# Second layer's gate modulation moved between the layers, second weight tile loaded last, low-weight parts between the row tiles

## The chip, the cores and the metric

One Trainium2 chip, one core of it. The kernel is one launch that computes the whole step. The metric is the device time of the launch in microseconds, lower is better.

## The reference

Two layers of a decoder trunk, over one prompt of 512 rows and eight decode rows (520 rows together), model width 1024. Cut to what matters:

```
for l in range(2):
    mod = silu(c) @ ada_w[l] + ada_b[l]            # (9, 3072): 1 prompt + 8 decode vectors
    shift, scale, gate = split(mod, 3)             # 1024 each
    h = rms_norm(x, norm_g[l]) * (1 + scale) + shift
    proj = h @ w_in[l]                             # 1024 x 7944
    oA, oB, oC, oD = four mixer branches of proj's first columns   # each 256 wide
    up = stack([oA, oB, oC, oD]) @ w_up[l]         # four products to width 1024
    merged = sum_n(sigmoid(proj gate columns n) * up_n)
    x = x + gate * (merged @ w_out[l])
y = rms_norm(x, final_g)
```

`shift` and `scale` of a layer are needed before its first product; `gate` is needed only where the layer's output is added to x.

## The kernel before, in words

All activations lie transposed: 128 of the 1024 (or 256) channels on the partitions, the 520 rows along the free axis. A "row tile" below is one of the KT = 8 groups of 128 channels of h. Each product of w_in and w_out is done in parts for precision: a weight tile (128 output columns, 1024 deep, 512 KB) is loaded into a ring of three places (`ring`, filled by SP), ScalarE copies it to a rounded high part (`w_hi`, `split`, `first_split`), GpSimd computes the low part (`w_lo`). h has a high part (`h_hi`, ScalarE) and a low part (`h_lo`, VectorE). `product` then has 12 parts (PARTS) for one weight tile: parts 0 to 7 take row tile p with the high weights against h_hi and h_lo (four matmuls), parts 8 to 11 take the low weights of two row tiles against h_hi (four matmuls). After the last part ScalarE evacuates the bank (`evac`) and splits the tile two places further on.

Order on every engine is written out by hand: each engine has one instruction stream, and named semaphore tracks (`STEPS`, at the end of the file) count its steps. All transfers of a layer go through SP's one queue, in the order of the list `L.tiles`. A layer does the projections, the four branches (their small products are mixed with the remaining projection and gate tiles), then a tail: `up` 18 to 31, and eight output tiles `out` 0 to 7. The tanh of each gate tile is written out to memory and brought back (`scr_tanh`) for its `up`; the weights of an up (`upw`, 128 KB) are in a ring of three, reloaded when an up is done (`load_up`).

The modulation: silu(c) is in `c32`. A piece of `ada_w` is 256 rows by 512 columns (512 KB, in the ring); `ada_products` multiplies it with c32 (four fp32 matmuls), four pieces make one set of 512 columns, ScalarE copies the sums out (`modrow`) and `mod_columns` turns them into columns of the modulation. Layer 0's shift and scale are computed at the start (`ada0`, `mod0`, blocks 0 to 3 of 2 MB each in places of their own, in the order 0, 2, 1, 3, the first two giving the first half of the channels). Layer 0's tail holds 24 pieces: eight for its own gate, one after each of up 20, 22, 24, 26, 28, 29, 30 and 31, and sixteen for layer 1's shift and scale, two or three after each of the output tiles 0 to 5. Layer 1's tail holds eight, for its own gate, after the same ups.

At the start of layer 0, SP issues blocks 0 and 2, weight tile 0, block 1, weight tile 1, block 3, weight tile 2 and then x's save and the constants. TensorE takes block 0 and 2, their columns, block 1, and then goes through row tiles 0 to 3 for weight tiles 0 and 1 side by side, block 3, the columns, the first two low parts of both weight tiles, row tiles 4 to 7, and the rest of the low parts. ScalarE splits weight tiles 0 and 1 before it computes the first h_hi. In layer 1 the eight row tiles are followed by all low parts.

Between the layers: after output tile 7 come the sum of squares (`square_sums`, in two parts), its logarithm and exponential on ScalarE, and the first row tile on VectorE and ScalarE.

Of the kernel before, what the change touches and what calls it, by code (L numbers as in the profile page):

```python
# [18 lines left out]
P = 128  # L19
# [58 lines left out]
def build_program(nc, a, o, order):  # L78
# [8 lines left out]
    with ctx:  # L87
# [112 lines left out]
        s_ada0 = [sem(f"ada_in{c}") for c in range(8)]  # L200
        pe0, act0, dve0 = (track(n) for n in ("pe0", "act0", "dve0"))
# [19 lines left out]
        class Layer:  # L221

            def __init__(self, n):
# [15 lines left out]
                self.n_ada = 24 if n == 0 else 8  # L239
                self.up_piece = {k: m for m, k in enumerate((20, 22, 24, 26, 28, 29, 30, 31))}  # L240
# [37 lines left out]
        LAND = [RA[:, 2], RA[:, 3], ws[:, 16], ws[:, 17]]  # L278

# [107 lines left out]
        def _(sp):  # L387
# [23 lines left out]
            ada_loads(1)  # L411
            first_load(sp, 1, LAYERS[0], 0)
            ada_loads(3)
# [13 lines left out]
        def _(act):  # L427
# [15 lines left out]
            first_split(act, 1, LAYERS[0])  # L443
# [28 lines left out]
        def _(pe):  # L472
# [35 lines left out]
            ada0(pe, 2)  # L508


        for layer, L in enumerate(LAYERS):
# [53 lines left out]
            def _(sp):  # L565
# [63 lines left out]

                def load_up(n):  # L630
# [23 lines left out]
                def before(kind, n):  # L654
# [47 lines left out]
                    elif (kind, n) == ("ada", 2):  # L702
# [7 lines left out]
                    elif (kind, n) == ("ada", 5):  # L710
# [4 lines left out]
                if layer == 0:  # L715
                    sp.wait_ge(s_zero, 2)
                    sp.wait_ge(*pe0.at("mod", 3))
                sp.dma_start(srow[:, :], a["state_rows"][layer]).then_inc(s_st, 16)
# [10 lines left out]
                for x in L.tiles:  # L729
# [192 lines left out]
            def _(pe):  # L922
# [100 lines left out]
                pe.wait_ge(*ap.at("proj", 9))  # L1023
                crow_rows([RA[:, j] for j in range(7)], 0, 0, pa.step("crow"))
# [495 lines left out]

                def turn(d):

                    pe.wait_ge(*dve_f.at("xg", d))
# [42 lines left out]
                for e in range(KT):  # L1566
# [7 lines left out]
                    if layer and e == 0:  # L1574
                        mods(1)
# [6 lines left out]
                if layer == 0:  # L1582
# [1181 lines left out]
```

## Time and profile before

| what | value |
|---|---|
| three runs | 1366.55, 1369.79, 1371.92 us; median 1369.79 |
| the profiled execution | 1368.49 us, span 1366.6 us |
| mean granted TensorE clock | 0.987 |
| TensorE busy | 1318.0 us, 96% of the span |
| VectorE busy | 623.3 us, 46% |
| ScalarE busy | 450.7 us, 33% |
| GpSimd busy | 375.0 us, 27% |
| DMA queue of SP | 159.00 MB, 42.6% of 16 engines |

The span is the time from the first to the last instruction of the profiled execution; its own time is that with what lies around it. Shares of busy time are averages over stages that differ. Names of engines in the rows: PE is TensorE (PEld its weight loads), DVE VectorE, ACT ScalarE, POOL GpSimd, SPq the queue of the engine that issues transfers. A row's bracket gives the idle time of the engine before the instruction and what ended it.

### The profile page before, as it was taken

The page shows a single profiled execution, that of the slowest core. Times are in us where ns is not written, and L with a number is a line of the kernel's source. Part 1 is how long each engine was busy: PE and PEld are TensorE (multiplying, and loading weights), DVE is VectorE, ACT ScalarE, POOL GpSimd, SP SyncE. Part 2 cuts the span into 40 slices and gives each one's busy share as a digit, 9 for nine tenths or more (in the row PEclk, how much of TensorE's full clock was granted, in tenths as well). Part 3 has the DMA queues.
Part 4 walks back from the last instruction along what each step waited for, and adds up shares of the span by engine and source line. Part 5 has one row for each costly group of instructions (what it writes and reads, how often), then busy time and mean ns, then how long its engine had stood idle before and what let it go on. Part 6 is the DMA issues. An engine that isn't in the chain of part 4 may idle for free.

```text
span 1366.6 us, 39992 instructions
## 1 busy us (share of the span) xinstructions
PE 1318.0 (96%) x18150; PEld 1190.6 (87%) x18150; DVE 623.3 (46%) x1166; ACT 450.7 (33%) x742; POOL 375.0 (27%) x286
## 2 busy tenths in 40 slices
PE   5899999999999999999989999999999999999996
PEld 4799999889899999887779999999988899988796
DVE  3557524317234336756252961332643242565643
ACT  3334422234322235231243353222442223532223
POOL 0244422223222232220333452212331222322121
PEclk9899999999999999999999999999999999999998
DMA  9833231216331272578853433212373224545932
GB/s 309 265 89 93 68 93 49 65 49 138 106 86 49 65 141 78 159 195 260 286 170 79 106 78 82 62 35 70 76 165 96 52 57 92 126 133 134 290 120 94
DMA packets 275932, 162.59 MB, mean 119 GB/s; under 512 B 86102, under 2 KB 244922, under 8 KB 275252
## 3 DMA queue, kind: packets, MB, share of 16 engines
q1 hardware_dynamic: 275220, 159.00, 42.6%
q8 instruction: 143, 2.34, 0.7%
q10 hardware_dynamic: 544, 1.05, 0.2%
q14 instruction: 25, 0.20, 0.0%
HBM read 135.25 MB, written 24.89 MB: 117 GB/s over the span
## 4 chain that ended last, share of the span: by engine, by line
PE 90%; DMA 3%; DVE 2%; ACT 2%; SPq 2%; issue 1%; ACTq 0%; DVEq 0%
PE psA L942 40%; PE psA L950 20%; PE psA L992 8%; PE psB L884 2%; PE psB L868 2%; DMA ring<-in_ada_w 2%; PE psB L888 1%; PE psB L1073 1%; PE psB L315 1%; PE psB L1083 1%; DMA ring<-in_w_in 1%; SPq L400 1%; PE psB L852 1%; PE psB L1311 1%; PE psB L800 1%
## 5 line engine op out<-in xcount | busy, mean ns | idle before, releaser
L778 POOL TENSOR_TENSOR w_lo<-ring,w_hi 128x512 fp32r<-128x512 f32 x248 | 331.1, 1356 | 823.6 <-ACT w_hi L1607 779.1
L942 PE MATMUL psA<-h_hi,w_hi 128*128 128x260 f32 x1984 | 426.8, 297 | 10.4 <-DVE h_lo L2034 9.4
L942 PE MATMUL psA<-h_lo,w_hi 128*128 128x260 f32 x1984 | 401.9, 284 | 0.8 <-issue 0.8
L942 PEld LDWEIGHTS psA<-h_hi,w_hi 128*128 128x128 f32 x1984 | 307.4, 190 | 30.4 <-issue 19.1
L942 PEld LDWEIGHTS psA<-h_lo,w_hi 128*128 128x128 f32 x1984 | 308.7, 190 | 1.4 <-issue 1.1
L950 PE MATMUL psA<-h_hi,w_lo 128*128 128x260 f32 x1984 | 273.6, 286 | 0.0
L950 PEld LDWEIGHTS psA<-h_hi,w_lo 128*128 128x128 f32 x1984 | 249.0, 187 | 6.8 <-issue 3.0
L1607 ACT CAST w_hi<-ring 128x1024 fp32r<-128x1024 f32 x120 | 123.9, 1032 | 10.0 <-DMA ring<-in_w_in 9.9
L893 ACT COPY ws<-psB 128x128 f32<-128x128 f32 x80 | 21.4, 268 | 190.0 <-PE psB L868 162.6
L1637 ACT ACTIVATE tg<-psA 128x520 f32<-128x520 f32 x48 | 28.9, 602 | 119.5 <-PE psA L950 119.3
L901 DVE COPY_PREDICATED tg<-tmask,psB 128x128 f32<-128x128 uint8 x40 | 14.2, 355 | 102.6 <-PE psB L888 58.9
L901 DVE COPY_PREDICATED ws<-tmask,psB 128x128 f32<-128x128 uint8 x40 | 14.2, 356 | 79.2 <-PE psB L888 42.6
L778 POOL TENSOR_TENSOR rb_lo<-RB,w_hi 128x512 fp32r<-128x512 f32 x16 | 21.7, 1380 | 98.4 <-ACT w_hi L1607 98.4
L778 POOL TENSOR_TENSOR rb_lo<-RB,ra_lo 128x512 fp32r<-128x512 f32 x16 | 21.0, 1338 | 49.1 <-ACT ra_lo L1607 49.1
L992 PE MATMUL psA<-RB,upw 128*128 128x260 f32 x128 | 31.8, 393 | 1.7 <-DVE psA L2100 0.9
L1622 ACT COPY RA<-psA 128x520 f32<-128x520 f32 x18 | 10.7, 593 | 64.0 <-PE psA L950 64.0
L992 PEld LDWEIGHTS psA<-RB,upw 128*128 128x128 f32 x128 | 23.2, 190 | 9.5 <-issue 4.9
L2300 DVE SCALAR_TENSOR_TENSOR ws<-RD,parT,ws 128x511 f32<-128x511 f32 (+2 forms) x36 | 30.9, 924 | 0.7 <-ACT ws L1810 0.6
L992 PE MATMUL psA<-RA,upw 128*128 128x260 f32 x128 | 30.7, 385 | 0.0
L992 PE MATMUL psA<-RD,upw 128*128 128x260 f32 x128 | 29.9, 384 | 0.8 <-DVE RA L2101 0.8
L992 PE MATMUL psA<-RC,upw 128*128 128x260 f32 x128 | 30.0, 387 | 0.3 <-DVE psA L2100 0.3
L950 PE MATMUL psA<-merged_hi,rb_lo 128*128 128x260 f32 x224 | 29.1, 282 | 0.0
(504 smaller groups left out, 1973.3 us busy)
## 6 DMA issues: line engine op xcount, KB each, us to landing
ring<-in_w_in SPq DMA_DIRECT2D x122, 512.0 KB, 4.3
ring<-in_ada_w SPq DMA_DIRECT2D x32, 512.0 KB, 5.9
scr_tanh<-tg SPq DMA_DIRECT2D x48, 260.0 KB, 4.6
upw<-in_w_up SPq DMA_DIRECT2D x64, 128.0 KB, 3.5
RB<-in_w_out SPq DMA_DIRECT2D x16, 512.0 KB, 3.8
RA<-scr_tanh SPq DMA_DIRECT2D x30, 260.0 KB, 3.8
ws<-scr_tanh SPq DMA_DIRECT2D x24, 260.0 KB, 4.2
xT<-scr_x SPq DMA_DIRECT2D x8, 520.0 KB, 4.7
```

The lines of the kernel that those rows point to most:

```text
L315: last = nc.tensor.matmul(out[g:g + 32, 0:256], c32[:, k0 + k, :], piece[:, k, 256 * f:256 * f + 256], start=start, stop=stop)
L778: nc.gpsimd.tensor_tensor(tile_part(RL[s][:, k], (kind, n)), tile_part(RS[s][:, k], (kind, n)), tile_part(HS[L.hslot[q]][:, k], (kind, n)) ...
L868: last = nc.tensor.matmul(meet(z0[pr, cols], lv, 0), At[pr, q, cols], meet(T4[pr, q, cols], lv, 0), start=True, stop=True)
L884: nc.tensor.matmul(meet(z0[pr, cols], lv, 0), V4[pr, q, cols], meet(Y4[pr, q, cols], lv, 0), start=True, stop=True)
L893: nc.scalar.copy(meet(q64(Y), lv, 0), meet(q64(psB[:, 2, 0:256]), lv, 0)).then_inc(*ta.step("y"))
L901: nc.vector.copy_predicated(meet(q64(T), lv, 0), bc(meet(tmask[:, lv, :], lv, 0), 1, 4), meet(q64(psB[:, 2, 0:256]), lv, 0))
L942: nc.tensor.matmul(out(h), HS[L.hslot[q]][:, p, 0:m], cols(part(p), h), start=(p == 0 and part is hi), stop=False)
L950: last = nc.tensor.matmul(out(h), RL[s][:, k, 0:m], cols(hi(k), h), start=False, stop=(k == KT - 1))
L992: last = nc.tensor.matmul(out(hf), upw[:, idx % UP_RING, i, :], outs[MERGE[idx][0]][:, i, hf * HALF:(hf + 1) * HALF], start=(i == 0), stop ...
L1607: nc.scalar.copy(tile_part(HS[L.hslot[q]], SPLIT[q]), tile_part(RS[s], SPLIT[q])).then_inc(*aw.step("hi"))
L1637: A(half(th_tile(idx)), psA[:, b:b + 2, 0:HALF], ACT.Tanh, scale=0.5).then_inc(*am.step("th"))
L2300: last = STT(out[:, t, sh:SEQ], raw[:, t, 0:SEQ - sh], par(wname, tap * n + t), out[:, t, sh:SEQ], mult, add)
```

## The change

Five edits, in one.

1. Start of layer 0: SP issues the fourth modulation block (block 3) ahead of weight tile 1. ScalarE splits tile 1 only after it has copied out the last two blocks' sums, so after the first half's h_hi. TensorE takes row tiles 0 to 3 for weight tile 0 alone, then blocks 1 and 3 and the columns, then two low parts of tile 0, row tiles 0 to 3 of tile 1 and its two low parts.
2. In both layers the low parts of the first two weight tiles come between the row tiles: after every second row tile, the part that needs the two.
3. Layer 1's tail has no pieces of `ada_w` any more. SP loads them in layer 0's tail, into places of their own (`LATE`, eight places of 1024 columns): two after up 15, two after up 20, one after up 25, three after output tile 0, as soon as that place is free.
4. TensorE multiplies them at layer 0's end: two before the sum of squares, six behind it. ScalarE copies the sums in layer 1 after h_hi, TensorE forms the columns after the first two weight tiles, VectorE adds the bias and halves them before the projections' shift.
5. Small stores that stood with pieces 2 and 5 in layer 1 go to output tiles 2 and 3; SP's first loads of layer 1 wait for the last late piece.

```diff
+        LATE = [two(t, at) for t, at in ((ws, 10), (RC, 2), (RB, 6), (ws, 0), (RC, 0), (RB, 4), (RA, 2), (ws, 16))]
+        late_bank = lambda b: psB[:, 1 - b, 0:256]
+        late_mods = psB[:, 0, 256:512]
-                self.n_ada = 24 if n == 0 else 8
+                self.n_ada = 24 if n == 0 else 0
...
             ada_loads(1)
+            ada_loads(3)
             first_load(sp, 1, LAYERS[0], 0)
-            ada_loads(3)
             first_load(sp, 2, LAYERS[0], 0)
...
             first_split(act, 0, LAYERS[0])
-            first_split(act, 1, LAYERS[0])
...
             mod0(pe, 1)
-            ada0(pe, 2)
...
+                def load_late(*ms):
+                    for m in ms:
+                        sp.dma_start(wide(LATE[m]), a["ada_w"][1, 256 * (m % 4):256 * (m % 4) + 256, 2048 + 512 * (m // 4):2560 + 512 * (m // 4)]
+                                     .rearrange("(k p) c -> p k c", p=P)).then_inc(s_late[m], 16)
...
-                    elif (kind, n) == ("ada", 2):
+                    elif (kind, n) == (("ada", 2) if layer == 0 else ("out", 2)):
...
-                    elif (kind, n) == ("ada", 5):
+                    elif (kind, n) == (("ada", 5) if layer == 0 else ("out", 3)):
...
+                else:
+                    sp.wait_ge(*LAYERS[0].TR["pe_f"].at("ada", 31))
                 sp.dma_start(srow[:, :], a["state_rows"][layer]).then_inc(s_st, 16)
...
+                    if layer == 0 and x == ("up", 15):
+                        sp.wait_ge(*dn.at("gated", 2))
+                        load_late(0, 1)
+                    if layer == 0 and x == ("up", 20):
+                        sp.wait_ge(*dn.at("gated", 3))
+                        load_late(2, 3)
+                    if layer == 0 and x == ("up", 25):
+                        sp.wait_ge(*pm.at("gate", 23))
+                        load_late(4)
+                    if layer == 0 and x == ("out", 0):
+                        sp.wait_ge(*merged_at(31))
+                        load_late(5, 6, 7)
...
-                for p in range(KT):
-                    if layer == 0 and p == KT // 2:
-                        ada0(pe, 3)
-                        mod0(pe, 2)
-                        mod0(pe, 3)
+                if layer == 0:
+                    proj(0, range(KT // 2))
+                    ada0(pe, 2)
+                    ada0(pe, 3)
+                    mod0(pe, 2)
+                    mod0(pe, 3)
+                    proj(0, (KT, KT + 1))
+                    proj(1, range(KT // 2))
+                    proj(1, (KT, KT + 1))
+                for p in range(KT // 2 if layer == 0 else 0, KT):
+                    for idx in range(2):
+                        proj(idx, [p])
+                    if p % 2:
                         for idx in range(2):
-                            proj(idx, (KT, KT + 1))
-                    proj(0, [p])
-                    proj(1, [p])
-                for idx in range(2):
-                    proj(idx, range(KT + 2 if layer == 0 else KT, PARTS))
+                            proj(idx, [KT + p // 2])
+                if layer:
+                    for b in range(2):
+                        pe.wait_ge(*LAYERS[0].TR["act_f"].at("modrow", 6 + b))
+                    for b in range(2):
+                        mod_columns(late_mods, b, modrow[:, b, :]).then_inc(*LAYERS[0].TR["pe_f"].step("mod"))
...
+                def late(m):
+                    pe.wait_ge(s_late[m], 16)
+                    if m == 4:
+                        pe.wait_ge(*dve_f.at("mod2"))
+                        pe.wait_ge(*dve_f.at("parT"))
+                    ada_products(late_bank(m // 4), wide(LATE[m]), 2 * (m % 4), m % 4 == 0, m % 4 == 3).then_inc(*pe_f.step("ada"))
...
-                    if layer and e == 0:
-                        mods(1)
...
                 if layer == 0:
+                    late(0)
+                    late(1)
                     square_sums().then_inc(*pe_f.step("ss"))
+                    for m in range(2, 8):
+                        late(m)
...
                         mod_rows0(act, 3)
+                        first_split(act, 1, LAYERS[0])
...
+                if layer:
+                    for b in range(2):
+                        act.wait_ge(*LAYERS[0].TR["pe_f"].at("mod", 4 + b))
+                        act.wait_ge(*LAYERS[0].TR["pe_f"].at("ada", 27 + 4 * b))
+                        nc.scalar.copy(modrow[:, b, :], late_bank(b)).then_inc(*LAYERS[0].TR["act_f"].step("modrow"))
                 evac(0, 1)
...
+                if layer:
+                    f0 = LAYERS[0].TR
+                    dve.wait_ge(*f0["pe_f"].at("mod", 7))
+                    did(f0["dve_f"], "modT", T_(modT[:, 16:24, :], late_mods[:, 0:72].rearrange("p (r s) -> p r s", r=8), bc(par("ada_b", 16, 8), 2, 9), add), 1)
+                    did(f0["dve_f"], "gate", S_(modT[:, 16:24, :], modT[:, 16:24, :], 0.5, None, mult), 1)
                 dve.wait_ge(*ap.at("proj", 9))
```

## Rows read from the trace of the kernel before

**Rows 1.** The page's part 4: share of the chain by line.
```profile
PE psA L942 40%; PE psA L950 20%; PE psA L992 8%; PE psB L884 2%; PE psB L868 2%; DMA ring<-in_ada_w 2%; PE psB L888 1%; PE psB L1073 1%; PE psB L315 1%; PE psB L1083 1%; DMA ring<-in_w_in 1%; SPq L400 1%; PE psB L852 1%; PE psB L1311 1%; PE psB L800 1%
```

**Rows 2.** Busy time by stretch: length, PE, PEld, DVE, ACT, POOL, clock, DMA share, GB/s.
```profile
606.50:646.80 40.30, 39.27 (x250) 28.60 (x249) 24.51 (x36) 9.89 (x15) 4.97 (x4) 1.00 0.82 259
646.80:700.30 53.50, 51.38 (x468) 45.16 (x468) 16.51 (x39) 12.60 (x18) 20.12 (x14) 1.00 0.84 280
1269.40:1308.00 38.60, 37.61 (x234) 28.27 (x232) 24.41 (x36) 9.89 (x15) 4.96 (x4) 1.00 0.72 233
```

**Rows 3.** Chain of waits, 20 to 60 us: start, length, what.
```profile
21.97 12.39 DMA ring<-in_w_in
...
35.33 0.72 ACT h_hi L1683
...
37.19 5.92 PE psA L942 x32
...
44.98 1.13 PE psB L322 x8
...
50.34 0.67 DVE h_lo L2034
...
58.41 1.68 PE psA L942 x12
```

**Rows 4.** Timeline of layer 0's start: start, length, engine, line, operation.
```profile
29.20 0.75 DVE L2044 SCALAR_TENSOR_TENSOR hT<-RC,G,tg 128x512 f32<-128x512 f32 x1
...
32.64 1.93 PE L315 MATMUL psB<-RB,cond_padded 128*32 128x256 f32 x16 [1.71 <-DMA RB<-in_ada_w]
...
49.73 0.51 PE L942 MATMUL psA<-h_hi,w_hi 128*128 128x260 f32 x2 [1.63 <-DVE h_lo L2034]
```

**Rows 5.** Busy time by stretch, as rows 2, where the clock is down.
```profile
32.00:36.00 4.00, 1.93 (x16) 0.59 (x16) 0.00 (x0) 1.62 (x3) 0.00 (x0) 0.50 1.06 377
...
52.00:56.00 4.00, 4.00 (x24) 4.00 (x24) 1.86 (x6) 0.42 (x1) 0.00 (x0) 0.63 1.07 205
...
705.00:710.00 5.00, 1.27 (x6) 1.30 (x7) 4.64 (x9) 2.30 (x4) 0.85 (x1) 0.69 0.39 103
```

**Rows 6.** Timeline between the layers, TensorE.
```profile
702.40 1.14 PE L1538 MATMUL psB<-ws,cst 128*128 128x260 f32 x4 [1.10 <-ACT ws L1986]
...
708.73 0.77 PE L942 MATMUL psA<-h_hi,w_hi 128*128 128x260 f32 x2 [5.18 <-DVE h_lo L2034]
...
718.75 3.99 PE L950 MATMUL psA<-h_hi,w_lo 128*128 128x260 f32 x32
...
722.58 0.45 PE L942 MATMUL psA<-h_hi,w_hi 128*128 128x260 f32 x2
```

**Rows 7.** Timeline of layer 1's tail.
```profile
1289.56 3.77 PE L992 MATMUL psA<-RB,upw 128*128 128x260 f32 x16
...
1293.58 0.70 DVE L2100 SCALAR_TENSOR_TENSOR psA<-RA,psA 128x520 f32<-128x520 f32 x1
...
1301.84 1.94 PE L1550 MATMUL psA<-merged_hi,ra_lo 128*128 128x260 f32 x14
```

**Rows 8.** Layer 0's tail: stretches; the transfer issued at 614.60; timeline, chain; waits.
```profile
585.00:587.50 2.50, 2.50 (x24) 2.30 (x22) 1.14 (x3) 0.00 (x0) 0.00 (x0) 1.00 0.04 3
650.00:652.50 2.50, 2.50 (x23) 2.50 (x22) 0.00 (x0) 0.77 (x2) 2.19 (x2) 1.00 0.99 369
...
upw<-in_w_up SPq DMA_DIRECT2D x1, 128.0 KB, 4.1
...
618.88 1.99 PE L992 MATMUL psA<-RB,upw 128*128 128x260 f32 x8
...
646.95 6.94 DMA ring<-in_ada_w
...
654.50 0.51 PE L942 MATMUL psA<-merged_hi,w_hi 128*128 128x260 f32 x2
...
PE psB L315 <- DMA ring<-in_ada_w: 1.9, 4, 0.7
```

More of the change, by code:

```diff
@@ L200, in build_program @@
         s_ada0 = [sem(f"ada_in{c}") for c in range(8)]
+        s_late = [sem(f"late_ada_in{m}") for m in range(8)]
         pe0, act0, dve0 = (track(n) for n in ("pe0", "act0", "dve0"))
@@ L238, in __init__ @@
                     "pe_n", "act_n", "dve_n", "pe_m", "act_m", "dve_m")}
-                self.n_ada = 24 if n == 0 else 8
-                self.up_piece = {k: m for m, k in enumerate((20, 22, 24, 26, 28, 29, 30, 31))}
+                self.n_ada = 24 if n == 0 else 0
+                self.up_piece = {k: m for m, k in enumerate((20, 22, 24, 26, 28, 29, 30, 31)) if m < self.n_ada}
                 self.out_pieces = [[m for m in pieces if m < self.n_ada] for pieces in
@@ L1023, in _ @@
                 pe.wait_ge(*ap.at("proj", 9))
+                if layer:
+                    pe.wait_ge(*LAYERS[0].TR["dve_f"].at("gate", 1))
                 crow_rows([RA[:, j] for j in range(7)], 0, 0, pa.step("crow"))
@@ L1519, in _ @@
                         ada(L.up_piece[idx])
+                def late(m):
[4 more added lines that the diff above has]
+                    ada_products(late_bank(m // 4), wide(LATE[m]), 2 * (m % 4), m % 4 == 0, m % 4 == 3).then_inc(*pe_f.step("ada"))
                 def turn(d):
+                    if d == 0:
+                        pe.wait_ge(*TR["act_c"].at("hrow"))
                     pe.wait_ge(*dve_f.at("xg", d))
@@ L2130, in _ @@
                 did(dd, "gc", v.tensor_tensor_scan(bg[32:36, :], cc("reset", 32, 36), g1, 0.0, mult, add))
+                if layer:
+                    f0 = LAYERS[0].TR
+                    dve.wait_ge(*f0["pe_f"].at("mod", 7))
+                    did(f0["dve_f"], "modT", T_(modT[:, 16:24, :], late_mods[:, 0:72].rearrange("p (r s) -> p r s", r=8), bc(par("ada_b", 16, 8), 2, 9), add), 1)
+                    did(f0["dve_f"], "gate", S_(modT[:, 16:24, :], modT[:, 16:24, :], 0.5, None, mult), 1)
                 dve.wait_ge(*ap.at("proj", 9))
@@ L2530, in _ @@
                 mods = lambda lo, n: psB[:, 0, 9 * lo:9 * (lo + n)].rearrange("p (r s) -> p r s", r=n)
-                dve.wait_ge(*pe_f.at("mod", 1))
-                did(dve_f, "modT", T_(modT[:, 16:24, :], mods(0, 8), bc(par("ada_b", 16, 8), 2, 9), add))
-                did(dve_f, "gate", S_(modT[:, 16:24, :], modT[:, 16:24, :], 0.5, None, mult))
+                if layer == 0:
+                    dve.wait_ge(*pe_f.at("mod", 1))
+                    did(dve_f, "modT", T_(modT[:, 16:24, :], mods(0, 8), bc(par("ada_b", 16, 8), 2, 9), add))
+                    did(dve_f, "gate", S_(modT[:, 16:24, :], modT[:, 16:24, :], 0.5, None, mult))
                 def sum_squares(k):
@@ L2603 @@
     'dve0': 'c_zero silu_c xs c parT selh hrows spread x x x x x x x x ssp modT G modT G sel tmask'.split(),
-    'pe_f0': 'st ada ada ada ada ada ada mod ada ada ada ada mod ada ada ada ada mod ada ada ada ada mod ada ada ada ada mod ada ada mod par ss'.split(),
-    'act_f0': 'hh hhd hh hh hh hh hhd hh hh hh lam_abs lam_z expA modrow modrow sq modrow sq modrow sq sq modrow sq modrow sq sq sq lnx rs'.split(),
-    'dve_f0': 'hg hr hs hd hs hld hl hs hl hs hl hl hg hr hs hd hs hld hl hs hl hs hl hl zero der lam1 lam2 lam3 lam4 lam5 lamm13 lama13 lamm11 lama11 lamm9 lama9 lamm7 lama7 lamm5 lama5 lamm3 lama3 lamm1 lama1 lam6 lam_y lam_sp stT modT gate acc acc acc acc acc acc parT mod2 G'.split(),
+    'pe_f0': 'st ada ada ada ada ada ada mod ada ada ada ada mod ada ada ada ada mod ada ada ada ada mod ada ada ada ada mod ada ada mod par ada ada ss ada ada ada ada ada ada mod mod'.split(),
+    'act_f0': 'hh hhd hh hh hh hh hhd hh hh hh lam_abs lam_z expA modrow modrow sq modrow sq modrow sq sq modrow sq modrow sq sq sq lnx rs modrow modrow'.split(),
+    'dve_f0': 'hg hr hs hd hs hld hl hs hl hs hl hl hg hr hs hd hs hld hl hs hl hs hl hl zero der lam1 lam2 lam3 lam4 lam5 lamm13 lama13 lamm11 lama11 lamm9 lama9 lamm7 lama7 lamm5 lama5 lamm3 lama3 lamm1 lama1 lam6 lam_y lam_sp stT modT gate acc acc acc acc acc acc parT mod2 G modT gate'.split(),
     'pe_a0': 'crow lora lora kks kkb bsum gram gram tr tr z gram y z y z gram y z y z tr y tr z z gram y x1 z u y o z gram y x1 z u y o z tr y tr z z gram y x1 z u y o z gram y x1 z u y o z tr y tr z z y x1 z u y o z y x1 z u y o z y z x1 u o x1 u o mt'.split(),
```

6 lines of the change are left out of this document (3 added, 3 removed).

## Prediction

> **What bounds the kernel now.** I read the chain of waits first: it runs through TensorE almost all the way, most of it the projection's products of line 942 and their low-weight parts of line 950 [rows 1]. So a change counts only by what it adds to or takes from TensorE's queue, and by the waits in that queue. Then I read the busy time by stage. In layer 0's tail TensorE is busy 39.3 of 40.3 us and 51.4 of 53.5 us, with the DMA engines at 0.82 and 0.84; in layer 1's tail 37.6 of 38.6 us, DMA 0.72 [rows 2]. TensorE's queue is therefore full, but layer 0's tail has little DMA to spare. Last I read three places where it does stand still: the start, the step between the layers, and single waits for transfers in the tails.
>
> **Start of layer 0.** The chain goes through the landing of the second weight tile at 34.36 (issued 21.97, 12.39 us); ScalarE then splits it, and only at 35.33 starts the first h_hi, though VectorE had written that row tile at 29.95 [rows 3, 4]. The change takes this split out of the way: h_hi starts at about 30.1, 5.3 us earlier, and the first product at 31.9 instead of 37.19. VectorE paces the row tiles at 1.33 us (two operations of 0.67 [rows 3]), so tile 0's first four parts are through at 36.3. Only then does TensorE take the third block of the modulation. Half a block takes 1.93 us at the low clock (0.50 from 32 to 36 [rows 5], x16 in 1.93 [rows 4]), so 0.97 at the high one. With the clock back soon after 38, the third block ends near 39.2 and the fourth near 41.2; its data land some 1.7 us earlier, being now ahead of a 512 KB tile. ScalarE's copy and the last columns take 1.1 us (44.98 + 1.13 = 46.1 before [rows 3]), so they end at 42.3, 3.8 us earlier. VectorE and ScalarE then need 3.6 us until the second half's first row tile (46.1 to 49.73 [rows 3, 4]), to 45.9. TensorE fills this: low parts of tile 0 (8 matmuls of 0.12 [rows 6], 0.96), four parts of tile 1 (1.93), its low parts (0.96), to 46.2. Four row tiles for two weight tiles (3.9) and two pairs of low parts (1.9) end at 52.0. Both tiles now end together, so evacuation and split of the third tile (1.9 us after the first tile's end, measured between the layers: 718.75 + 2.0 to 722.58 [rows 6]) lie open for 1.3 us: the third tile starts at 53.3 against 58.41 [rows 3], 5.1 us earlier. If the clock stays low until 41.3, as it did, it is 3.7. I take 4.8; ends 3.0 and 5.5. The tile "ba" is then asked for behind the masks and state rows that are still landing; it is wanted at 59.1, which I cost at nothing, 1 us if that cover fails.
>
> **Layer 1's tail.** Out go eight pieces of the gate modulation among the last ups, two sets of columns, and two small VectorE operations before the first output tile (beside the products, nothing). Pitch of two ups without a piece: 3.77 us from 1289.56 with the tail of the last matmul in it [rows 7], so 1.83 to 1.85 each. Fourteen ups by 1.83 are 25.6; out_first from 1301.84 to its end at about 1307.7 is 5.85. Together 31.5 of the 38.6 us of this stretch [rows 2], a gain of 7.1. VectorE is late next: in the last ups it has three operations of 0.7 per up [rows 7], some 2.0 us with their overlap against 1.83, about 0.3 us in all that shows. An up's weights must now land within 3.6 us of their issue; without the pieces nothing queues ahead of them. I take 6.8, ends 5.5 and 7.3. Four small stores that SP issued beside pieces 2 and 5 move ahead of the third and fourth output tiles, issued before their wait ends: nothing.
>
> **Between the layers.** Eight pieces at 0.48 (half of a half block's 0.97) are added. Two go before the square sums into TensorE's wait of 1.10 us for the last square, six into the wait of 5.18 us for h_lo [rows 6]; both hide them. SP's state loads wait for the last piece, 4 us; what follows on SP is next wanted at about 720, so nothing. Then the low parts come between the row tiles: the stretch of 64 high and 32 low matmuls is 11.5 us at the high clock from 708.73, 720.2, plus the open 1.4 of evacuation and split (the columns, 0.8, lie in it): the third tile at 722.0 against 722.58, a gain of 0.6. But the work is now bound by TensorE's clock instead of by VectorE. The clock was down here (0.69 [rows 5]), and it was down from 52 to 56 (0.63 [rows 5]) after an idle of only 1.63 us before 49.73 [rows 4]; 2.2 us of idle remain now. Some 3 us at the low clock, as there, cost 1.5. I take a loss of 0.8, ends a gain of 0.7 and a loss of 2.
>
> **Layer 0's tail pays.** The 4 MB that layer 1's tail no longer loads are loaded here: eight loads of 512 KB. At 369 GB/s [rows 8] one takes 1.4 us of all DMA engines.
> - Pieces 0 and 1, near 581, go into an almost idle DMA (0.04 [rows 8]): nothing.
> - Pieces 2 and 3, after up 20 (612.5), stand ahead of the weights of up 24. These were issued at 614.60, took 4.1 us to 618.7, and up 24 began at 618.88 [rows 8]: no slack. 2.8 us less a little idle: 2.6.
> - Piece 4, after up 25: slack of 1 us and more in the ups behind: 0.3.
> - Pieces 5 to 7, after output tile 0, go ahead of the ring's pieces 11 and 12. The latter landed at 646.95 + 6.94 = 653.89 and the next tile's products began at 654.50 [rows 8]: no slack, 4.2 us. In exchange later waits shrink: there are 1.9 us of them for pieces [rows 8], of which 1.1 come back: 3.1.
> - Both standstills are longer than the 1.63 us after which the clock fell [rows 4], so I add 1.5 for matmuls at half rate; ends 0 and 3.
> Sum 7.5, ends 3 and 10.
>
> What row and rule say on the queue: the latencies in this tail grow with what was issued just before (4.1 us for 128 KB, 6.94 for 512 KB behind three others [rows 8]). The Trainium skill, page "DMA: Bandwidth & Descriptors", section "Two DMAs through the same engine are not ordered", has descriptors within one queue of one engine start in order. By that rule no small load passes a late piece, and the stalls stand; if small loads passed, the cost would be near nothing, which is the first rival. This speaks against the change, and the trace agrees.
>
> **Sum.** Against the profiled execution (1368.49, of which 1366.6 span and 1.9 around it): -4.8 - 6.8 + 0.8 + 7.5 = -3.3, 1365.2. The median of the three runs is 1.3 above it; from 1369.79 I forecast 1366.5.
>
> **Rivals.**
> 1. The late loads are hidden: then 3.3 + 7.5 = 10.8 us are gained, 1359.0. For it: DMA is not full (0.82). Against it: the landings that end just before their use.
> 2. The start gives only about 1.5 us: the third and fourth blocks now run after products at the low clock and the clock stays low to the last columns, or "ba" or the masks come late. Gain 3.3 less 3.3: 1369.8. For it: clock 0.50 from 32 to 36 [rows 5]. Against it: TensorE is busier there than before.
> 3. Slower: late loads starve the output tiles. This phase refills three ring places per tile; if the 4.2 us of backlog is never worked off, so that every following group of pieces waits for it again, each of three more groups costs some 3 us, 9 in all with half-rate matmuls: 1366.5 + 9 = 1375.5. It decides once a group's loads are issued less than 7 us before use (6.94 was the landing). Against it: a standing TensorE lets the DMA drain, and no wait for a piece was longer than 0.7 us before [rows 8].
> 4. The tail of layer 0 costs 4 instead of 7.5: no clock loss, and DMA works off a part of each backlog while TensorE is at the matmuls before. 1363.0.
>
> **Chances.** Forecast 0.55, rival 1 0.12, rival 2 0.13, rival 3 0.05, rival 4 0.15. Half a per cent, 6.8 us, is about what a measurement tells from no change here. Faster by more (below 1362.9): rival 1, half of rival 4 and a little of the forecast, 0.24. Slower by more (above 1376.6): part of rival 3, 0.04. Within: 0.72. Range 1360.5 to 1371.0: it leaves out most of rival 1 and rival 3.
>
> **What would show it.** Right: first L942 product near 32; third tile's first product near 53; no L315 in layer 1's tail, which ends its first output tile about 7 us sooner after up 18; TensorE idle near up 24 of layer 0 waiting for upw, and 3 to 4 us after output tile 1 waiting for ada_w, with a lower granted clock behind them. Wrong: no such waits (rival 1), or the columns' end in layer 0 later than 44 (rival 2), or idle of over 2 us in each output group (rival 3).

## The result, and the profile after

Changed kernel: 1373.64 us median of 9 runs (1371.6 to 1377.1); the kernel before beside it 1370.35 (1366.27 to 1372.41, 9 runs). Ratio 1.0038, 95% interval [1.0023, 1.0054]: slower by 5.2 us (3.2 to 7.4, at 1370 us). Forecast were 1366.5, range 1360.5 to 1371.0: outside, and on the other side. The profiled execution took 1372.27 us (span 1370.5) against 1368.49 and 1366.6. Busy times hardly moved (TensorE 1318.5 us against 1318.0), so the question is again one of waits and of the clock.

The chain of waits by engine. In the kernel before TensorE had 90% of it, VectorE 2% and DMA 3%: VectorE's share has grown. The products of lines 942 and 950 in [rows 1] are lines 964 and 972 now:

```profile
PE 88%; DVE 4%; DMA 3%; ACT 2%; SPq 1%; issue 1%; ACTq 0%; DVEq 0%
```

To see where the time went, take the same instruction in both traces and subtract its starts. The same was done for every experiment; the table gives the difference to the profiled execution before, in us (its own time in the first row). "Third tile" is its first product, "up 20, 31" are layer 0's ups, "squares" the first matmul of the square sums, "L1" layer 1's first product, "stT" VectorE's copy of that name in layer 1, "crow" the transposes of crow_rows in layer 1, "lora" the product behind them, "up 17'" and "out 0'" an up and the first output product of layer 1's tail, "end" the last matmul.

```
                       third        up    up                                 up      out
                       tile         20    31  squares  L1    stT  crow  lora  17'     0'    end
before (time)          58.4        610   637   700     709   746   770   782  1254   1302   1357
the change             -0.4       -2.3  -0.1  +5.3    +4.3  +3.7  +6.1  +7.6 +11.2   +4.7   +3.8
e1 gate early          -2.4       -1.8  +0.3  +7.6    +6.5  +7.4  +7.4  +7.4 +10.6   +3.8   +2.9
e2 late loads short    -0.7       -2.3  -3.6  -0.8    -1.9  -0.8  +1.5  +3.0  +7.4   +0.7   -0.3
e3 start undone        -1.5       -4.0  -0.3  +5.9    +4.8  +5.5  +7.9  +9.4  +9.8   +3.0   +2.0
e4 split first         -4.5       -4.0  -0.1  +5.7    +4.7  +5.4  +7.7  +9.2 +12.6   +6.0   +5.0
e5 late loads moved    -2.1       -2.2  -2.2  +2.4    +1.3  +1.9  +4.2  +5.8  +8.6   +1.7   +0.8
e6 e1 + e4 + e5        -4.9       -4.2  -3.6  +3.7    +2.7  +2.1  +2.1  +2.1  +3.8   -3.3   -3.5
e7 start alone         -2.2       -3.9  -4.2  -3.9    -3.9  -3.9  -3.9  -3.9  -4.6   -4.0   -4.0
e8 start alone, split  -4.0       -4.3  -4.6  -5.5    -5.5  -5.6  -5.6  -5.6  -6.2   -6.4   -6.9
e9 e1 + e4, spread     -4.3       -5.9  -6.0  -1.3    -2.3  -1.3  -1.3  -1.3  +0.8   -6.2   -7.1
e10 e9, low parts last -4.6       -0.9  -2.0  +2.9    +1.9  +2.6  +2.6  +2.6  +4.5   -2.5   -3.4
e11 e1 + e4, short     -4.4       -3.6  -4.1  -2.9    -4.0  -4.5  -4.5  -4.5  -3.1  -10.0  -10.6
e12 e9, old start      -0.8        0.0  +0.2  +8.3    +7.2  +6.7  +6.7  +6.7  +8.2   +1.2   +0.3
```

One profiled execution carries much chance, above all by where the clock falls: e9 and e10 run the same instructions up to layer 1 and stand 5.0 us apart at up 20; e3 and e12 have the kernel before's instructions up to up 15, and e3 is 4.0 us early at up 20 where e12 is at 0.0. So single entries are read together with the ratios below, or over several kernels at once.

**Start.** The timeline, as [rows 4]:

```profile
33.15 0.77 PE L964 MATMUL psA<-h_hi,w_hi 128*128 128x260 f32 x2 [3.73 <-DVE h_lo L2085]
43.78 1.31 DVE L385 SCALAR_TENSOR_TENSOR G<-modT,parT 128x36 f32<-128x36 f32 x1
43.76 2.52 POOL L800 TENSOR_TENSOR w_lo<-ring,w_hi 128x512 fp32r<-128x512 f32 x2 [4.65 <-ACT w_hi L307]
45.12 1.20 DVE L2092 TENSOR_TENSOR hT<-mg,G 128x32 f32<-128x32 f32 x1
49.17 0.51 PE L964 MATMUL psA<-h_hi,w_hi 128*128 128x260 f32 x2 [1.84 <-DVE h_lo L2085]
57.99 0.47 PE L964 MATMUL psA<-h_hi,w_hi 128*128 128x260 f32 x2 [1.24 <-ACT w_hi L1652]
```

The first product comes 4.0 us earlier (37.19 in [rows 3]), the third tile 0.4 (58.41 there). In between VectorE's G takes 1.31 us and hT 1.20; the same two took 0.20 and 0.19 before. Over all profiles (the table's first column) the third tile starts at 56.9 to 58.4 with the old start (the kernel before, e3, e12), at 56.0 to 58.0 with the new one (the change, e1, e2, e5, e7) and at 53.5 to 54.4 with the new one and ScalarE's swap of e4 (e4, e6, e8 to e11). By the means the new start is worth 0.8 us there, and 3.7 with the swap.

**Layer 0's tail.** The stretches of [rows 2], then the 4 us behind output tile 1, the waits from 600 to 705 us (total, times, longest), and the products that waited behind output tile 1:

```profile
608.00:648.50 40.50, 37.16 (x247) 27.37 (x247) 24.52 (x40) 6.17 (x11) 4.25 (x4) 1.00 0.88 294
648.50:704.00 55.50, 50.21 (x448) 43.74 (x448) 14.96 (x34) 12.60 (x18) 20.03 (x14) 0.97 0.85 287
...
657.00:661.00 4.00, 3.21 (x20) 2.39 (x19) 0.00 (x0) 1.82 (x3) 0.33 (x1) 0.57 1.09 363
```

```profile
PE psB L319 <- DMA ring<-in_ada_w: 5.3, 4, 3.1
PE psA L1014 <- DMA upw<-in_w_up: 1.8, 2, 1.1
PE psA L1014 <- DVE mg L2152: 1.6, 1, 1.6
```

```profile
656.37 0.64 PE L319 MATMUL psB<-ring,cond_padded 128*32 128x256 f32 x8 [3.13 <-DMA ring<-in_ada_w]
657.80 1.08 PE L319 MATMUL psB<-ring,cond_padded 128*32 128x256 f32 x8 [0.79 <-DMA ring<-in_ada_w]
```

Waits for pieces were 1.9 us in four, at most 0.7 [rows 8]; now 5.3 in four, at most 3.1, and the granted clock was 0.57 over the 4 us behind them: at the lower level of 1.2 GHz for most of the stretch, at 2.4 GHz for the rest.

**Between the layers** (as [rows 6]): the idle of 5.18 us is 2.48 now, and the clock stays high there. The first two late pieces stand ahead of the squares and the other six behind them; the second part of the squares, which waited 1.10 us for ScalarE before [rows 6], starts without a wait:

```profile
705.60 1.14 PE L1578 MATMUL psB<-ws,cst 128*128 128x260 f32 x4
706.65 1.14 PE L1581 MATMUL psB<-ws,cst 128*128 128x260 f32 x4
...
713.00 0.48 PE L964 MATMUL psA<-h_hi,w_hi 128*128 128x260 f32 x2 [2.48 <-DVE h_lo L2085]
...
724.87 0.96 PE L326 MATMUL psB<-sel_halves,ws 128*128 128x18 f32 x8
```

So the squares stand 5.3 us late, and 1.1 us of that is given back at once: their second part, and layer 1's first product, are 4.2 to 4.3 us late. In the table every kernel with late pieces shows this step of 1.1 us between "squares" and "L1", and e7 and e8, without them, do not. What layer 0's tail cost is therefore read at "L1".

**A new wait before crow_rows.** The chain of waits at 770 to 780 us, after (start, length, what):

```profile
773.64 1.24 DVE bg L2181
774.91 0.24 DVE modT L2186
...
775.17 1.11 DVE modT L2187
776.28 0.14 issue
776.42 1.26 PE psB L1021 x7
```

and the same place in the timeline of the kernel before, where TensorE's crow_rows (line 999) did not need VectorE's long chain and ran beside its last operation:

```profile
769.91 1.23 DVE L2130 TENSOR_TENSOR_SCAN bg<-cst,small_rows 4x520 f32<-4x520 f32 x1
...
770.37 0.93 PE L999 MATMUL psB<-cst,RA 128*11 128x128 f32 x7
```

The columns of the late gate modulation (`late_mods`) lie in the PSUM bank that crow_rows writes. So TensorE must wait until VectorE has read them, and VectorE reads them only behind a chain of 26 operations, most on small_rows. TensorE waits 2.2 us, and then the clock is low from 776.9 to 780.3 (0.66 below).

```profile
776.00:781.00 5.00, 4.58 (x26) 4.41 (x27) 4.93 (x6) 0.94 (x2) 1.44 (x2) 0.66 0.22 61
```

**Layer 1's tail** (as [rows 7]): no pieces stand among the ups any more. Up 17 is 11.2 us later than before, and out_first, the first output tile, only 4.7.

```profile
1293.83 12.76 PE L1014 MATMUL psA<-RB,upw 128*128 128x260 f32 x53
1306.53 1.94 PE L1593 MATMUL psA<-merged_hi,ra_lo 128*128 128x260 f32 x14
```

### The profile page after: what moved, and what is told of

The parts are those of the page before. It is cut to its first block, busy times and chain, and to the rows that moved or that the text cites. A ratio compares the mean times of both kernels' runs of the same rounds, so it can differ in the third digit from the quotient of the medians.

```text
span 1370.5 us, 40001 instructions
## 1 busy us (share of the span) xinstructions
PE 1318.5 (96%) x18150; PEld 1192.8 (87%) x18150; DVE 624.1 (46%) x1166; ACT 450.6 (33%) x742; POOL 373.8 (27%) x286
## 4 chain that ended last, share of the span: by engine, by line
PE 88%; DVE 4%; DMA 3%; ACT 2%; SPq 1%; issue 1%; ACTq 0%; DVEq 0%
PE psA L964 38%; PE psA L972 19%; PE psA L1014 7%; PE psB L890 2%; PE psB L906 2%; PE psB L910 1%; DMA ring<-in_ada_w 1%; PE psB L1106 1%; PE psB L319 1%; PE psB L1116 1%; DMA upw<-in_w_up 1%; PE psB L874 1%; PE psB L1344 1%; DMA hT<-in_x_prompt 1%; PE psB L1069 1%
```

## The experiments

Twelve kernels. Ratios are to runs of the kernel before on the same chip, and different groups ran on different chips, so the ratios are compared and not the medians.

| kernel | median us | ratio to before, 95% |
|---|---|---|
| the change | 1373.64 | 1.0038 [1.0023, 1.0054] |
| e1 gate early | 1371.14 | 1.0013 [0.9999, 1.0026] |
| e2 late loads short | 1366.42 | 0.9977 [0.9962, 0.9992] |
| e3 start undone | 1375.23 | 1.0042 [1.0027, 1.0057] |
| e4 split first | 1373.71 | 1.0027 [1.0009, 1.0045] |
| e5 late loads moved | 1369.87 | 1.0013 [0.9996, 1.0030] |
| e6 = e1 + e4 + e5 | 1360.91 | 0.9937 [0.9917, 0.9958] |
| e7 start alone, on before | 1365.79 | 0.9983 [0.9968, 0.9998] |
| e8 start alone, split first | 1366.24 | 0.9977 [0.9964, 0.9990] |
| e9 = e1 + e4, late loads spread | 1361.53 | 0.9945 [0.9928, 0.9962] |
| e10 = e9, layer 1's low parts last | 1362.66 | 0.9952 [0.9929, 0.9975] |
| e11 = e1 + e4, late loads short | 1361.35 | 0.9952 [0.9935, 0.9970] |
| e12 = e9 with the old start | 1366.85 | 0.9969 [0.9953, 0.9985] |

**e1: the new wait.** The two operations ahead of VectorE's long chain:

```diff
+                if layer:
+                    f0 = LAYERS[0].TR
+                    dve.wait_ge(*f0["pe_f"].at("mod", 7))
+                    did(f0["dve_f"], "modT", ...)
+                    did(f0["dve_f"], "gate", ...)
                 dve.wait_ge(*pe_f.at("st"))
                 did(dve_f, "stT", ...)
...
                 did(dd, "gc", v.tensor_tensor_scan(...))
-                if layer:
-                    (the same five lines)
```

> The changed kernel with one edit: VectorE's two operations on layer 1's gate modulation (modT, gate) stand ahead of the copy stT instead of behind the chain of small_rows operations (log1p to scan). Theory A (the new wait): TensorE's crow_rows waits 2.2 us for them and 1.7 us more are lost to a low granted clock from 776.9 to 780.3; both go, the lora products start 3.3 to 3.8 us earlier, time 1370.0 against 1373.6. Theory B (VectorE is the bound there anyway): the wait moves to the first lora products, which need VectorE's mix of RA's row 6 and ScalarE's tanh; only the 1.3 us of the two operations come back, time 1372.3. Theory C: wait and clock in the trace are hidden by slack later; 1373.6.

Its timeline and its busy time around the place (columns as [rows 2]); the second fence is the changed kernel's:

```profile
777.80 0.93 PE L1021 MATMUL psB<-cst,RA 128*11 128x128 f32 x7
```

```profile
768.00:785.00 17.00, 17.00 (x145) 16.90 (x144) 16.61 (x17) 5.46 (x8) 8.25 (x6) 1.00 0.40 101
```

```profile
768.00:785.00 17.00, 14.84 (x113) 14.46 (x112) 16.61 (x22) 4.88 (x8) 5.39 (x4) 0.90 0.35 89
```

No wait, clock 1.00, and TensorE is busy all of the 17 us. From stT to lora its distance to the kernel before stays +7.4, where the change lost 3.9. The ratio falls by 0.0025 (3.4 us, some 3 either way). Theory A holds by the trace; the ratios alone would also allow theory B's 1.3 us. Theory B, that VectorE binds there anyway, falls: VectorE is as busy (16.61) and nobody waits. The clock tells the same over all kernels: of the five profiles with this wait (the change, e2 to e5) all five show it low between 773 and 782, of the nine without it (the kernel before among them) none.

**e2: the bytes of the late loads.**

```diff
-                        sp.dma_start(wide(LATE[m]), a["ada_w"][1, 256 * (m % 4):256 * (m % 4) + 256, 2048 + 512 * (m // 4):2560 + 512 * (m // 4)]
+                        sp.dma_start(wide(LATE[m])[:, 0:1, 0:8], a["ada_w"][1, 256 * (m % 4):256 * (m % 4) + P, 2048 + 512 * (m // 4):2056 + 512 * (m // 4)]
```

> The changed kernel with its eight late loads cut from 512 KB to 4 KB each (leaves out: all but eight columns of one row block of each piece of layer 1's gate modulation; the products read what stood there before). Instructions, waits and places are the same, only the bytes go. Theory A (the bytes delay what is queued behind them, at TensorE): the waits near up 24 and up 29 of layer 0 and after output tile 1 go, 1.5 + 1.1 + 3.9 us with the clock, less 0.7 that stood in the kernel before: 5 to 6.5 us, time 1367.5. The prediction's sum says 7.5: 1366.1. Theory B (the stalls are given back later, or come from the queue's order and not its bytes): under 2 us, 1372.

```profile
PE psB L319 <- DMA ring<-in_ada_w: 2.3, 4, 0.8
```

All waits for up weights are gone, and those for pieces are close to those of the kernel before (1.9 us). The loads of 128 KB issued between 612 and 618 us landed after 3.3 to 4.0 us, in the change after 5.0 to 5.7. The ratio falls by 0.0061, 8.4 us (some 3 either way), the trace by 6.1 at "L1". That is theory A, and the prediction's 7.5 lies within the interval. Theory B falls.

**e3, e4, e7, e8, e12: the start.** e3 puts the old start into the change, e7 the new start into the kernel before. e4 and e8 swap two steps of ScalarE in it:

```diff
+                        first_split(act, 1, LAYERS[0])
                         mod_rows0(act, 2)
                         mod_rows0(act, 3)
-                        first_split(act, 1, LAYERS[0])
```

> The changed kernel with only the start of layer 0 as it was before (order of the loads, second weight tile split first, third block of the modulation ahead of the products, low parts of the two tiles at the end); layer 1 keeps its low parts between the row tiles. The prediction's step gave this part 4.8 us: 1378.4 if that is right. Theory A from the two traces (the start gained 4 us at the first product and lost them again at the second half's row tiles and at the split of the third tile): the part is worth 0.4 to 1.4 us, time 1374.0 to 1375.0. Theory B (the part is a loss): under 1373.

> The changed kernel with one swap on ScalarE in the start of layer 0: the second weight tile (landed 39.6) is split before the copies of the modulation rows (40.6 and 42.4), not behind them, so GpSimd computes its low part from about 40.7 to 43.2 instead of 43.8 to 46.3. Theory A (VectorE's G and hT took 1.31 and 1.20 us instead of 0.20 and 0.19 because GpSimd worked on the second tile's low part at the same time): they return to 0.2 each, the second half's first product comes 1.5 to 2.1 us earlier than 49.17, the third tile too, time about 1371.8. Theory B (the two are slow for another reason, such as the DMA writes to SBUF at that time): they stay over 1 us and the time is 1373.6; with the tile landing at 39.6 the row copy may then even wait and cost up to 0.5.

> The kernel before with only the start of layer 0 changed as in the change (order of the loads, split of the second tile, order of the modulation's blocks and of the products); no late loads, layer 1 as it was. The prediction's step gave 4.8 us: 1365.3. Theory A (the start itself brings 1.4 to 1.5 us at the third tile, since the second tile's split and the slow G and hT eat the rest): 1368.8. Theory B (what the start brings is taken again at the ups of layer 0, whose time is set by their loads even without the late ones): 1370.1.

> The same as the run with the start alone, with the second weight tile split ahead of the copies of the modulation rows. In the changed kernel this swap brought 3.2 us at layer 0's state rows (81.6), of which nothing was left at up 31. Theory A (the late bytes took it): without them 3 to 4.5 us arrive at the end, 1366.5. Theory B (layer 0's ups are bound by their own loads, late bytes or not): up 31 no earlier than before, 1370.

The timeline of e4:

```profile
40.62 2.52 POOL L800 TENSOR_TENSOR w_lo<-ring,w_hi 128x512 fp32r<-128x512 f32 x2 [2.30 <-ACT w_hi L307]
42.47 0.72 DVE L385 SCALAR_TENSOR_TENSOR G<-modT,parT 128x36 f32<-128x36 f32 x1
43.22 0.19 DVE L2092 TENSOR_TENSOR hT<-mg,G 128x32 f32<-128x32 f32 x1
46.26 0.51 PE L964 MATMUL psA<-h_hi,w_hi 128*128 128x260 f32 x2 [0.26 <-DVE h_lo L2085]
53.90 0.48 PE L964 MATMUL psA<-h_hi,w_hi 128*128 128x260 f32 x2 [1.25 <-ACT w_hi L1652]
```

GpSimd's two operations end at 43.14 now, G at 43.19 (0.72 us instead of 1.31), and hT takes 0.19 again. In the change GpSimd's two (1.26 each from 43.76) end at 45.02 and 46.28, VectorE's G at 45.09 and hT at 46.32: each VectorE operation ends when a GpSimd operation does. So theory A of e4 holds: the second tile's low part on GpSimd holds VectorE up. The Trainium skill, page "SBUF — State Buffer", section "SBUF: two separate sides", has VectorE operations with two SBUF inputs and GpSimd operations that read SBUF share a port pair that the first takes for its whole instruction. G and hT both read two SBUF tiles, and their ends agree with that. The gate operation of line 2187 reads only one; it took 1.10 us instead of 0.20 and ended at 776.27, where a GpSimd operation ended at 776.20. Whether it is of the two-port kind that the section also names, no run here shows.

The clock goes with this wait. In all five profiles with the new start and without the swap TensorE stood 1.8 to 1.9 us before the second half's first product, and the clock fell at 47.3 to 49.8 us. In the six with the swap it stood 0.4 us at most, and the clock did not fall there. With the old start it stood 1.6 us, and the clock fell in one of three. The second half's first product comes 2.9 us earlier in e4 than in the change, the third tile 4.1.

And yet e4's time is the change's (0.0011 less, within the intervals). Look at the table: in e4 the ups of layer 0 begin 4.0 us early at up 20, and up 31 is 0.1 early. The change goes from -2.3 to -0.1, e1 from -1.8 to +0.3. e3 has the old start, was 4.0 us early by chance, and goes to -0.3. Whatever lead there is, up 31 comes within 0.3 us of the old time: with the late pieces 2 to 4 in SP's queue the ups are paced by the queue. The waits of e4 from 600 to 705 us:

```profile
PE psB L319 <- DMA ring<-in_ada_w: 4.6, 3, 3.6
PE psA L1014 <- DMA upw<-in_w_up: 3.4, 2, 2.7
```

against 1.8 us for up weights in the change: TensorE comes sooner and waits longer. Without late bytes there (e2, e5 to e12) the difference at up 20 is kept to within 1.3 us. e3, the start taken out of the change, moves the ratio by 0.0004, 0.5 us (some 3 either way): theory A's size, and far from the 4.8 of the prediction. e7 and e8 show the start by itself: 2.3 us (0.3 to 4.4) and, with the swap, 3.2 us (1.4 to 4.9) by the ratios. Their profiles say 4.0 and 6.9, but the third tile's 0.8 and 3.7 fit the ratios better, and e8's profiled execution (1361.68) is the fastest of its twelve. Theory A of e8 holds (what arrives stays), theory B falls. e7's interval holds theory A's 1.5 and not the 4.8 of the prediction. e12 asks the same from the other side.

> The version with the gate operations early and the late loads spread, but with the start of layer 0 as it was before. It asks what the start is worth once the late bytes don't stand in layer 0's ups: undoing it in the changed kernel cost 1.6 us. Theory A (in the changed kernel the late bytes among the ups took what the start had gained; spread, it reaches the end): 3.5 to 4.5 us more than with the new start, 1365.5, and up 31 at 638 as before. Theory B (the start is worth 1.5 us whatever the loads do): 1363.

e12 against e9: 0.9969 against 0.9945, 3.3 us (some 3 either way), where undoing the start in the change cost 0.5 (e3, same width; the 1.6 in the text above compares medians of different chips). That is theory A's size, but the intervals don't part it from theory B. Nor does up 31 do so by itself (+0.2 against -6.0): e10, with the same instructions as e9 up to there, is at -2.0. What carries theory A is the third tile, 3.5 us later in e12, together with the four and the nine kernels above.

**e5, e9: where the late loads stand.**

In words, which late pieces SP loads where:

```
-  after up 20: 2, 3;  after up 25: 4;  after output tile 0: 5, 6, 7
+  e5: after up 31 (once merged): 2, 3, 5;  after ("ada", 15): 4;  after ("ada", 20): 6, 7
+  e9: after up 31: 2, 3;  after ("ada", 12): 5;  ("ada", 15): 4;  ("ada", 20): 6;  ("out", 5): 7
```

> The changed kernel with six of its eight late loads issued elsewhere: pieces 2, 3 and 5 once VectorE has merged the last up (640.2; the DMA share from 642 to 648 was 0.33), piece 4 behind the loads of output tile 2's pieces, 6 and 7 behind the last loads of the ring's pieces (684 to 690 was at 0.34 in the kernel before). The bytes are the same. Theory A (it is where the bytes queue, not how many there are): the ups run as with the 4 KB loads (3.5 us earlier at up 31) and the stall behind output tile 1 shrinks from 3.9 to 1 to 2 us: time 1369.0. Theory B (the tail from 600 to 705 has no room for 3 MB anywhere, so each load costs its 1.4 us where it stands): 1373 to 1374. Theory C (the start of the output phase is hit by three loads ahead of its first pieces): up 31 earlier, square sums no earlier.

> The changed kernel with three edits together: VectorE's two gate operations early, the second weight tile split first in the start, the six late loads moved. If the three are separate losses: 2.5 (measured for the first) + 0 to 2 (the second; its 3.2 us were gone at the ups of layer 0 while the late bytes stood there) + 4 (the third, if its theory A holds) less than 1373.6: 1366.0. If the late loads cost the same wherever they stand: 1370.5.

> As the run with all three edits, with the six late loads spread further: 2 and 3 once the last up is merged (not 5 with them), 5 behind the loads of output tile 1's pieces, 4 behind those of tile 2's, 6 behind the last piece of the ring, 7 behind output tile 7's weights. With three loads at once, TensorE waited 2.4 us at 652.1 for a ring piece queued behind them and lost 2.5 us more to the low clock until 659. Theory A (one late load per output tile fits into the queue's idle time of about 3 us per tile): this wait falls below 1 us, square sums 3 to 4 us earlier, time 1357.5. Theory B (the output phase has no room: each load shows its 1.4 us wherever it stands): 1360.9, as measured for the three at once.

Waits of e5, e6 and e9 for ring pieces from 600 to 705 us:

```profile
PE psB L319 <- DMA ring<-in_ada_w: 4.2, 4, 2.2
```

```profile
PE psB L319 <- DMA ring<-in_ada_w: 4.1, 4, 2.4
```

```profile
PE psB L319 <- DMA ring<-in_ada_w: 4.1, 6, 0.9
```

e5 gains 0.0025 (3.4 us, some 3 either way) over the change: the ups are free again, the output phase is not (from up 31 to "L1" it loses 3.5 us against 4.4). That is theories A and C each in part. e6 is 0.0101 under the change, 13.8 us, more than the 8.3 that e1, e4 and e5 bring one by one (0.0025 + 0.0011 + 0.0025). The intervals are as wide as this surplus, so it is not shown; the table shows what it would consist of: the start's gain counts only once the ups are free (up 31: -0.1 in e4, -2.2 in e5, -3.6 in e6). Spreading further (e9) cut the longest wait to 0.9 but made six of them; together 4.1 as before, and the time is e6's (intervals overlap). Theory B of e9 is nearer. By the profiles, too, 3 MB more in the output phase cost something wherever they stand: from up 31 to "L1" e5, e9 and e10 lose 3.5 to 3.8 us, e6 6.3 and e12 7.0 (10.2 us at the low clock there, against 3.4 in e5 and e9), against 1.7, 0.1 and 0.3 without the bytes (e2, e11, e7).

**e10, e11.**

e10's own step against e9; e11's is that of e2:

```diff
-                    if p % 2:
+                    if p % 2 and layer == 0:
...
                 if layer:
+                    for idx in range(2):
+                        proj(idx, range(KT, PARTS))
```

> As the run with the late loads spread, with layer 1's two first weight tiles as before: all eight row tiles, then their low parts. Theory A (low parts between the row tiles fill the time in which VectorE makes the next row tile, but evacuation and split of the third tile lie open instead): 0.5 to 1 us slower than with the low parts between. The prediction's step (a loss of 0.8 for the part as a whole, by the clock): equal or up to 1 us faster. Theory B (no difference that shows): within 0.3.

> The changed kernel with VectorE's gate operations early, the second tile split first, and all eight late loads cut to 4 KB (leaves out what the run with short late loads left out). It shows what the change is worth without the bytes and without the new wait. By adding: the start with the split first -4.6 at up 31 and -5.5 at the square sums, layer 1's tail -5.5 to -6.5, between the layers -1: 11 to 13 us under the kernel before, 1357. If the start's gain is taken again between the ups and the square sums even without the bytes (the queue's idle time there is what it takes from): 1360 to 1361.

e10 differs from e9 by 0.0007, 1 us in the expected direction and far inside the intervals: the times don't settle it. The table says more. From "L1" to "stT" e10, whose clock stayed high there, loses 0.8 us to the kernel before; the four kernels with the low parts between and the clock high (the change, e6, e11, e12) gain 0.5. So the low parts between the row tiles are worth 1.3 us by the traces, a little over theory A's size.

e11's ratio (0.9952) is no better than e9's with all bytes in, against my 1357; by its profile it is 3.5 us ahead of e9. Here profile and times differ, and I go by the times: the profiled execution of e11 (1357.85) is the fastest of its eight, 3.5 us under their median. What the spread bytes still cost is under some 2.5 us. For the same reason e6's profile (1365.07, the slowest of six, median 1360.91) says too little for it.

**The best version.** e6 and e9 beat both kernels: 8.6 us (5.8 to 11.4) and 7.5 us (5.2 to 9.9) under the kernel before.

## Why the prediction was wrong

By its own steps, with the trace's differences:

- **Start, -4.8: measured -0.4** in this profile, 0.8 by the means. The first product and the end of the columns came as forecast: 31.9 and 42.3 against means of 32.3 and 42.2 over the five profiles (33.15 and 43.41 in the change's own, where the prompt's rows landed 0.95 us later than in the kernel before). The step failed where it said "VectorE and ScalarE then need 3.6 us until the second half's first row tile": they took 5.8 in all five, since I had moved GpSimd's low part of the second tile beside them and counted it as nothing. Then up to 1.7 us went to the clock (low 49.8 to 53.2), which the step had at its high level. With the swap of e4 the start is worth 3.7. Of rival 2's two causes neither was it, though its size was near.
- **The sum as such.** I added the start to the tail as if both reached the end. They don't: what arrives early at up 20 is spent waiting for up weights, because the late pieces make SP's queue the pace there (the change, e1, e3, e4). In the change as it stands the start is worth 0.5 us (e3), alone 2.3 (e7), with the swap 3.2 (e8). So even a start of 4.8 would not have come through.
- **Layer 0's tail, +7.5: measured +6.6** in this trace (from -2.3 at up 20 to +4.3 at "L1"), 8.4 by e2. The mechanism was right, the two standstills and the low clock behind the second included; ups 2.2 (I had 2.6 + 0.3), output phase 4.4 (3.1 + 1.5 of clock). That the total fits is partly luck, for it depends on the lead: with 4.0 us at up 20 (e3, e4) this stage took 8.7 to 8.8, and with the 4.8 that I forecast it would have taken more than 7.5. Rivals 1 and 4 fall. So does rival 3: behind the one stall after output tile 1 the following groups lost nothing more (the product behind it is 4.3 us late, layer 1's first product too).
- **Between the layers, +0.8: measured -0.6** in this trace ("L1" to "stT"). The step was right in both its branches, and the level of the clock was not mine to forecast: where it fell between 706 and 720 us (e1 to e5, e9) the kernels lost 0.6 to 1.1, where it stayed high (the change, e6, e11, e12) they gained 0.5; I had a loss of 0.8 and a gain of 0.6. All of them have the six pieces in TensorE's idle time, so these did not keep the clock up; why it fell in some is open. (My sum of this step has a slip, 720.2 and 1.4 make 721.6 and not 722.0.)
- **crow_rows: not in the sum, measured +3.9.** 2.2 us of wait and 1.7 of clock. The diff shows the added wait in plain sight; I named what queued behind other waits and not this one. Taking it away brought 3.4 us (e1).
- **Layer 1's tail, -6.8: measured -7.5** (from +11.2 at up 17' to +3.8 at the end; -7.3 to -8.0 in all eleven kernels that have it), a little beyond the end at 7.3.
- **Not in the sum: +3.7 in the middle of layer 1** (lora +7.6, up 17' +11.2). The clock was low from 1032.9 to 1036.3 and 1046.5 to 1049.9, where it wasn't before. Nine of ten experiments with the late pieces show at least one such stretch (3.4 to 10.2 us at the low clock between 1020 and 1050, 1.4 to 4.4 us lost from "lora" to "up 17'"), the kernel before, e3, e7 and e8 none. I find no cause: in the 10 us ahead of the fall TensorE does the same work in the change and, 2.6 us later, in e3, whose clock stayed up:

```profile
1022.60:1027.60 5.00, 4.54 (x40) 4.21 (x40) 1.24 (x1) 0.40 (x1) 0.00 (x0) 1.00 0.02 5
1027.60:1032.60 5.00, 5.00 (x27) 3.02 (x25) 1.93 (x2) 1.54 (x2) 2.49 (x2) 1.00 0.68 181
1032.60:1037.60 5.00, 5.00 (x30) 5.00 (x30) 2.27 (x8) 0.00 (x0) 0.00 (x0) 0.66 0.01 4
```

```profile
1025.20:1030.20 5.00, 4.52 (x40) 4.18 (x40) 1.24 (x1) 0.43 (x1) 0.00 (x0) 1.00 0.02 5
1030.20:1035.20 5.00, 5.00 (x27) 3.04 (x25) 1.93 (x2) 1.54 (x2) 2.49 (x2) 1.00 0.67 178
1035.20:1040.20 5.00, 5.00 (x42) 4.98 (x43) 2.27 (x8) 0.00 (x0) 0.00 (x0) 1.00 0.04 10
```

The first fence is the change's, the second e3's. This stays open.

Together: -0.4 at the start, -1.9 (most of it because the kernel before had a low clock from 362 to 366 that the change hadn't; over the fourteen profiles such a fall comes and goes near there in kernels with the same instructions, so it is chance as far as I see), +6.6, -0.6, +3.9, +3.7, -7.5 make the +3.8 of the last matmul. Of the distance to the forecast, some 4 us each are the start, the wait before crow_rows with its low clock, and the unexplained loss in the middle of layer 1; the other terms together came out 4.9 us better than forecast.

## What to carry to other kernels

A gain ahead of a stretch that a queue paces is not a gain: before adding terms, ask at each later stage whether TensorE or the queue sets its end once the change's own bytes are in it. When results are moved to places of their own, read who writes those places next and what the reader stands behind on its engine: here two operations of 1.3 us, placed behind a chain of 26, cost 3.4 us and were free ahead of it. Test the parts together as well as one by one: here 3.4 + 1.5 + 3.4 us separately were 13.8 together, though the intervals are too wide to show a surplus. Before reading a difference off two traces, look at two kernels with the same instructions in that stretch: here they were up to 5 us apart. And end a stage at an instruction that the change has not moved: here the two late pieces ahead of the squares shift that marker by 1.1 us.

## What was not expected of the hardware

- A VectorE operation on 36 or 32 elements a partition took 1.31 and 1.20 us instead of 0.20 and 0.19 beside a GpSimd operation of 1.26 us, and ended with it. With GpSimd's work moved ahead they took 0.72 and 0.19 in e4.
- The granted clock fell to its lower level in one kernel and not in another after the same 10 us of TensorE work, so one profile can be off by 1.7 us for each such stretch of 3.4 us.
